# Folding the token transform of the Fourier branch by symmetry

## The chip, the cores and the metric

The kernel runs as one program on 1 core of one Trainium2 chip. Times are device microseconds (us) of one execution, lower is better. TensorE (PE) does the matrix products, VectorE (DVE), ScalarE (ACT) and GpSimd (POOL) the element-wise work, and SyncE (SP) issues the large loads. The engines meet only through semaphores.

## The reference, cut to what matters

The program is one layer of a diffusion trunk over 512 latent tokens of width 1024 (plus 256 context tokens), all in float32. A normalised, modulated input is projected into four branches: global attention, a Fourier branch, windowed attention and a gated recurrence. Each branch result is multiplied by its own matrix, weighted by a gate, and summed; then come an output projection, and a mixture of 16 experts with 2 experts per token. The change touches only the Fourier branch:

```
def fourier_mix(u):                       # u: (1, 512 tokens, 256 features)
    b_, l_, _ = u.shape
    g = u.astype(jnp.float32).reshape(b_, l_, F_GROUPS, F_GROUP_W)     # 4 groups of 64 features
    y = jnp.real(jnp.fft.fft2(g, axes=(1, 3), norm='ortho'))           # tokens and features
    return y.reshape(b_, l_, -1).astype(u.dtype)
...
y_f = fourier_mix(fu)                     # fu: 256 of the columns of h @ w_in
```

The real part of this two-dimensional transform is a sum of two products: for each group the features are multiplied by a 64 x 64 table of cosines and by one of minus sines, and the two results are then multiplied along the tokens by a 512 x 512 table of cosines and one of sines and added.

## The kernel before, in words

Each engine runs a list written out by hand. On TensorE the order is: transposes of the input, first modulation products, the input projection (30 groups of tokens or features by 512 columns, `proj`), the gated recurrence between them, then 32 gate steps. A gate step (`gate`, or `gate_rows` for a part of it) computes one 128-feature block of one branch: eight products of 128x128 by 128x512 for the gate itself, two more for the branch's projection. ScalarE takes the tanh of the gate (`tanh`, L1099), VectorE multiplies it with the branch's projection (`gated`, L1422). Steps 0 to 7 belong to the recurrence's branch, 8 to 15 to the Fourier branch, then come the two attention branches. Steps 0 to 3 run ahead of the Fourier transform, 4 to 6 behind it. Then TensorE transposes queries and keys (`turn`, L463) and goes on to 16 attention units, with the remaining gate steps spread through them, then to the output projection, the router, and 16 experts.

The Fourier transform lies between gate steps 3 and 4, and has two stages on TensorE (all its products are recorded at the helper's line L460):

- First stage, over features: for each of 4 tiles of 128 tokens, the transposed features `fuT` (2 blocks of 128 features by 512 tokens, which stand in `yT[:, 1]`) are the stationary operand, and 256 columns of the constant table `tab` the moving one: 8 products of 256 columns. The result goes to two PSUM banks by turns, and ScalarE copies it (L1010, `copy`) to `gcs`, 4 copies of 128x512.
- Second stage, over tokens: for each of 2 feature blocks, 4 token tiles times 2 tables (cosine, sine) accumulate in one bank: 16 products of 512 columns. The moving operand is `dftL`, the two 512 x 512 tables, 2 MB, which SP loads (L400) as soon as the recurrence is done (`yG_ready`), ahead of the weights of gate steps 4 to 7. ScalarE copies each bank to `yT[:, 1]`.

VectorE's list over the same stretch is a loop of 7 rounds: in rounds 0 to 5 it normalises queries and keys of one token tile (squares, a sum, a root that GpSimd computes at L1694, two multiplications; L1432 to L1436), and in each round it then does `gated(t)`. GpSimd rotates the normalised rows of tiles 0 to 3 (L1715 to L1720) between these roots. TensorE's transposes of queries and keys wait for all of that (`rope_done`, `qk_norm`) and for `yF_ready`. SP's next loads behind `dftL` are the weights of gate steps 4 to 7 and 8 to 11.

What touches the order: a matmul of float32 leaves two records in the trace, a transpose leaves one. Buffers in the arena are reused by hand; `dftL` and `gcs` stand where the recurrence had its scratch rows.

Of the kernel before, what the change touches and what calls it, by code (L numbers as in the profile page):

```python
# [12 lines left out]
ALU = mybir.AluOpType  # L13
# [4 lines left out]
P = 128  # L18
D = 1024
KD = D // P  # L20
SEQ, CTX = 512, 256
XT, CT = SEQ // P, CTX // P
# [20 lines left out]
DFT = LOW + 16  # L43
# [55 lines left out]
def build(nc, A, out):  # L99
    ctx = ExitStack()  # L100
    with ctx:
# [3 lines left out]
        def sem(name):  # L105
            return ctx.enter_context(nc.semaphore(name))


        tab = sb("tab", [P, TABW])
# [27 lines left out]
        def region(at, *shape):  # L137
            n = int(np.prod(shape))
            v = arena[:, at:at + n]
            if len(shape) == 1:  # L140
                return v
            names = "abcd"[:len(shape)]
            return v.rearrange(f"p ({' '.join(names)}) -> p {' '.join(names)}", **dict(zip(names, shape)))

        SLOT = (KD + 2) * CW
        R_RING, R_HT, R_HC, R1 = 0, 15360, 19456, 21504
# [5 lines left out]
        yT = region(R_YT, NB, 2, SEQ)  # L152
        fuT = yT[:, 1]
# [32 lines left out]
        Pr = region(R1, 2, 768)  # L186
        PT = region(R1 + 1536, 2, 768)

        dftL = region(R1, 2, XT, SEQ)
        gcs = region(R1 + 4096, XT, 512)  # L190

        merged = region(R_G + 6656, KD, SEQ)
        th = region(R_HC, 2, SEQ)
# [29 lines left out]
        ps = ctx.enter_context(nc.psum_tensor("ps", [P, 8, 512], F32))  # L223
# [15 lines left out]
        dft_in, wb_in, xr_in, out_done = sem("dft_in"), sem("wb_in"), sem("xr_in"), sem("out_done")  # L239
# [5 lines left out]
        pj_mm, pj_done, qk_zero = sem("pj_mm"), sem("pj_done"), sem("qk_zero")  # L245
# [2 lines left out]
        qkinT_done, qinT_ready, kinT_ready, hgrn1_done = sem("qkinT_done"), sem("qinT_ready"), sem("kinT_ready"), sem("hgrn1_done")  # L248
        kv_done, state_step = sem("kv_done"), sem("state_step")
        att_done, attm_ready, o_done, o_read, yG_ready = sem("att_done"), sem("attm_ready"), sem("o_done"), sem("o_read"), sem("yG_ready")  # L250
        fgc_done, gcs_ready, yF_done, yF_ready = sem("fgc_done"), sem("gcs_ready"), sem("yF_done"), sem("yF_ready")
        qk_norm, rope_done = sem("qk_norm"), sem("rope_done")
        qkT_mm, qkT_ready = sem("qkT_mm"), sem("qkT_ready")
        sc_done, neg_ready, p_ready, ps_ready, pt_mm, pt_act, pt_dve, pv_done, y_copied = (
# [81 lines left out]
        def _(sp):  # L336
# [60 lines left out]
            for n in range(5, second_gate):  # L397
                load(n)
            sp.wait_ge(yG_ready, XT)
            sp.dma_start(dftL, A["dft_long"].rearrange("c (s p) t -> p c s t", p=P)).then_inc(dft_in, 16)  # L400
            load(second_gate)
            load(second_gate + 1)
            load(second_gate + 2)
# [54 lines left out]
        def _(pe):  # L458
            def mm(o, l, r, start, stop):
                return nc.tensor.matmul(o, l, r, start=start, stop=stop, skip_group_check=True)  # L460
# [259 lines left out]
            for g in range(1, 4):  # L720
                gate(g)

            for t in range(XT):
                if t >= 2:
                    pe.wait_ge(gcs_ready, t - 1)
                for ft in range(2):
                    last = mm(ps[:, 2 + 2 * (t % 2), ft * 256:(ft + 1) * 256], fuT[:, ft, t * P:(t + 1) * P],
                              tab[:, DFT:DFT + 256], True, True)
                last.then_inc(fgc_done, 1)
            pe.wait_ge(gcs_ready, XT)  # L730
            pe.wait_ge(dft_in, 16)
            for ft in range(2):
                for s in range(XT):
                    for c in range(2):
                        last = mm(ps[:, 2 + 2 * ft, :], gcs[:, s, ft * 256 + c * P:ft * 256 + (c + 1) * P],
                                  dftL[:, c, s, :], s == 0 and c == 0, s == XT - 1 and c == 1)
                last.then_inc(yF_done, 1)
            for g in range(4, 7):
                gate(g)
# [217 lines left out]
        def _(act):  # L957
# [51 lines left out]
            def copy(o, i):  # L1009
                return A_(o, i, ACT.Copy)  # L1010
# [91 lines left out]
                take_y(j, 2 + 2 * j)  # L1102
            for g in range(4):
                tanh(g)
            for t in range(XT):
                act.wait_ge(fgc_done, t + 1)
                copy(gcs[:, t, :], ps[:, 2 + 2 * (t % 2), :]).then_inc(gcs_ready, 1)
            for ft in range(2):
                act.wait_ge(yF_done, ft + 1)
                copy(yT[:, 1, ft, :], ps[:, 2 + 2 * ft, :]).then_inc(yF_ready, 1)  # L1110
            for g in range(4, 7):
                tanh(g)

# [1 line left out]
            for j in range(7):  # L1115
                act.wait_ge(qkT_mm, j + 1)
                B = ps[:, 2 + j % 2, :]
                if j < 4:
                    last = copy(qT[:, j, :], B)
# [93 lines left out]
        def _(dve):  # L1213
# [203 lines left out]
            def gated(g):  # L1417
                b, half, j, n = gates[g]
                dve.wait_ge(th_ready, g + 1)
                if g >= 10:  # L1420
                    dve.wait_ge(merged_add, g - 9)
                V.scalar_tensor_tensor(merged[:, half * 4 + j, :] if g < 8 else gtmp[:, g % 2, :], th[:, g % 2, :], 1.0,  # L1422
                                       ps[:, gate_bank(g)[0] + 1, :], ALU.add, ALU.mult).then_inc(gm_ready, 1)


            dve.wait_ge(yG_ready, XT)
            for t in range(7):
                if t < NT:
                    dve.wait_ge(pj_done, min(27 + t, len(groups)))
                    X = qk[:, t]  # L1430
                    sq = nsq.rearrange("p (h e) -> p h e", e=HD)
                    link(V.tensor_tensor(sq, X, X, ALU.mult))  # L1432
                    link(V.tensor_reduce(stat[:, 40:52], sq, AX.X, ALU.add))
                    rsqrt(stat[:, 40:52], stat[:, 40:52], 1.0 / HD)
                    link(V.tensor_tensor(X, X, stat[:, 40:52].unsqueeze(2).broadcast_to([P, 12, HD]), ALU.mult))
                    V.tensor_tensor(X, X, gain12[:, :, :], ALU.mult).then_inc(qk_norm, 1)  # L1436
                gated(t)


            def pt_copy(u):  # L1440
# [390 lines left out]
```

## Time and profile before

| what | value |
|---|---|
| median of 3 runs | 935.75 us (933.47 to 936.21) |
| profiled execution, its own time | 938.09 us |
| its span, first to last instruction | 936.1 us |
| mean granted TensorE clock | 0.971 |
| TensorE busy (matmul) | 874.8 us, 93% of the span |
| VectorE / ScalarE / GpSimd busy | 382.1 / 198.7 / 123.4 us |
| read from and written to memory | 128.36 and 12.58 MB |

The profiled execution takes 1.99 us more than its span and lies 2.34 us above the median. Engines overlap, so the busy times don't add up to the span. The whole program ran once for this profile; the rows further down have their starts in us from the start of the span.

### The profile page before, as it was taken

How to read it: one execution, taken by the hardware profiler on the slowest of the kernel's cores; microseconds unless marked ns; L12 is line 12 of the kernel's file. 1: busy time of each engine (PE TensorE's matmuls, PEld its weight loads, DVE VectorE, ACT ScalarE, POOL GpSimd, SP SyncE). 2: the span in 40 equal slices, each digit the busy share in tenths (PEclk: the TensorE clock that was granted, in tenths of full speed). 3: DMA queues.
4: the chain of work that ended last, by engine and by line, in shares of the span. 5: the costliest groups of instructions: out<-in, count | busy, mean ns of one | idle time of the engine just before them, and what ended most of it. 6: DMA issues, size and time to landing. Idle time of an engine off the chain costs nothing. (4 is left out here: it accounts for less than half of the span.)

```text
span 936.1 us, 9796 instructions
## 1 busy us (share of the span) xinstructions
PE 874.8 (93%) x3811; PEld 463.3 (49%) x3811; DVE 382.1 (41%) x795; ACT 198.7 (21%) x436; POOL 123.4 (13%) x109
## 2 busy tenths in 40 slices
PE   4999999999999999999999999999993899999992
PEld 3445475655844445555555554444453444444441
DVE  3239355552445224566576751101336322222221
ACT  3221366100011022223233320010120222111110
POOL 1000000000158200101111011110001022222211
PEclk9899999999999999999999999999995899999997
DMA  8852020300073025252442536204142489999952
GB/s 319 316 191 90 0 90 1 114 1 1 19 296 113 0 90 158 90 164 85 141 144 83 172 132 228 90 0 157 68 142 105 154 261 302 300 285 291 319 138 40
DMA packets 79727, 133.21 MB, mean 142 GB/s; under 512 B 7280, under 2 KB 40256, under 8 KB 79680
## 3 DMA queue, kind: packets, MB, share of 16 engines
q1 hardware_dynamic: 75072, 124.18, 39.0%
q0 software_dynamic: 4608, 8.40, 3.9%
q8 instruction: 30, 0.49, 0.2%
q14 instruction: 17, 0.14, 0.1%
HBM read 128.36 MB, written 12.58 MB: 151 GB/s over the span
## 5 line engine op out<-in xcount | busy, mean ns | idle before, releaser
L460 PE MATMUL ps<-arena 128*128 128x512 f32 (+8 forms) x2974 | 778.2, 451 | 17.2 <-DVE arena L1561 5.7
L460 PEld LDWEIGHTS ps<-arena 128*128 128x128 f32 (+6 forms) x2974 | 362.7, 167 | 383.4 <-issue 361.3
L1010 ACT ACTIVATE arena<-ps 128x128 f32<-128x128 f32 (+2 forms) x133 | 56.0, 445 | 188.9 <-PE ps L460 141.8
L463 PE MATMUL ps<-tab,arena 128*128 128x128 f32 x476 | 68.0, 287 | 13.5 <-DVE arena L1252 5.4
L463 PEld LDWEIGHTS ps<-tab,arena 128*128 128x128 f32 x476 | 58.6, 150 | 41.8 <-issue 34.0
L1422 DVE SCALAR_TENSOR_TENSOR arena<-arena,ps 128x512 f32<-128x512 f32 x32 | 22.0, 687 | 129.4 <-ACT arena L1099 129.2
L1729 POOL TENSOR_TENSOR arena<-arena 128x512 f32<-128x512 f32 x24 | 30.4, 1267 | 279.8 <-DVE arena L1422 279.8
L1694 POOL TENSOR_TENSOR stat<-stat,mhalf 128x1 f32<-128x1 f32 (+2 forms) x20 | 23.2, 1160 | 327.7 <-DVE stat L1227 327.5
L1099 ACT ACTIVATE arena<-ps 128x512 f32<-128x512 f32 x32 | 19.1, 597 | 198.7 <-PE ps L460 198.7
L1652 DVE TENSOR_TENSOR arena<-arena,ps 128x256 f32<-128x256 f32 x16 | 6.7, 421 | 105.9 <-ACT arena L1199 105.9
L1390 DVE SCALAR_TENSOR_TENSOR arena<-arena,cond 128x512 f32<-128x512 f32 x56 | 42.6, 761 | 2.3 <-PE ps L463 0.6
L1466 DVE TENSOR_REDUCE stat<-ps 128x1 f32<-128x768 f32 (+2 forms) x32 | 27.4, 855 | 24.8 <-PE ps L460 24.3
L1757 POOL DMA_INDIRECT out<-arena,tok_of x16 | 25.3, 1582 | 81.8 <-DVE arena L1647 76.0
L1647 DVE SCALAR_TENSOR_TENSOR arena<-ps,gate_of,arena 128x1024 f32<-128x1024 f32 x16 | 20.5, 1284 | 34.7 <-PE ps L460 34.7
L1303 DVE RECIPROCAL arena<-arena 128x256 f32<-128x256 f32 (+1 forms) x14 | 34.1, 2438 | 0.5
L1147 ACT ACTIVATE arena<-ps,stat 128x768 f32<-128x768 f32 (+2 forms) x32 | 25.9, 811 | 30.0 <-DVE stat L1471 29.5
L1748 POOL DMA_INDIRECT arena<-xd,tok_of x16 | 16.8, 1050 | 104.7 <-issue 88.7
L1193 ACT ACTIVATE arena<-ps,modc,A 128x128 f32<-128x128 f32 x64 | 24.1, 456 | 27.2 <-PE ps L463 27.2
L1199 ACT ACTIVATE arena<-ps 128x256 f32<-128x256 f32 x16 | 6.1, 384 | 110.4 <-PE ps L460 110.4
L1368 DVE SCALAR_TENSOR_TENSOR arena<-arena,edec,ps 128x64 f32<-128x64 f32 x92 | 18.2, 274 | 18.0 <-PE ps L460 18.0
L460 PEld LDWEIGHTS ps<-tab,arena 128*128 128x128 f32 x160 | 21.2, 191 | 7.6 <-issue 6.7
L1636 DVE TENSOR_SCALAR arena<-ps,A,modc 128x128 f32<-128x128 f32 x64 | 21.9, 403 | 4.0 <-PE ps L463 3.5
(144 smaller groups left out, 378.4 us busy)
## 6 DMA issues: line engine op xcount, KB each, us to landing
arena<-in_moe_w SPq DMA_DIRECT2D x32, 1024.0 KB, 10.1
arena<-in_w_in SPq DMA_DIRECT2D x12, 2048.0 KB, 8.8
arena<-in_mod_w SPq DMA_DIRECT2D x16, 1024.0 KB, 5.2
arena<-in_moe_w SPq DMA_DIRECT2D x32, 512.0 KB, 10.1
arena<-in_mod_w SPq DMA_DIRECT2D x4, 2048.0 KB, 16.5
arena<-in_w_out SPq DMA_DIRECT2D x2, 2048.0 KB, 8.0
arena<-in_x SPq DMA_DIRECT2D x4, 512.0 KB, 5.2
arena<-in_w_in SPq DMA_DIRECT2D x2, 1024.0 KB, 18.4
```

The lines of the kernel that those rows point to most:

```text
L460: return nc.tensor.matmul(o, l, r, start=start, stop=stop, skip_group_check=True)
L463: return nc.tensor.transpose(o, i, ident[0:n, 0:n])
L1010: return A_(o, i, ACT.Copy)
L1147: A_(Pr[:, a, 0:w], S[:, lo:lo + w], ACT.Exp, bias=stat[:, b3:b3 + 1], scale=SCALE, accum_out=stat[:, b3 + 1:b3 + 2]).then_inc(p_ready, 1)
L1193: last = A_(hgT[:, k, :], ps[:, 0, k * P:(k + 1) * P], ACT.Identity, bias=modc[:, 3 * KD + k, 0:1], scale=A2[:, k:k + 1])
L1303: link(V.reciprocal(e, e))
L1390: last = V.scalar_tensor_tensor(acc, modw[:, k, :], cond[:, k, 0:1], acc, ALU.mult, ALU.add)
L1422: V.scalar_tensor_tensor(merged[:, half * 4 + j, :] if g < 8 else gtmp[:, g % 2, :], th[:, g % 2, :], 1.0, ps[:, gate_bank(g)[0] + 1, :], ...
L1466: link(V.tensor_reduce(stat[:, b3:b3 + 1], S[:, lo:lo + w], AX.X, ALU.max))
L1694: G.tensor_tensor(o, o, mhalf[:, 0:o.shape[1]], ALU.pow).then_inc(root_done, 1)
L1729: G.tensor_tensor(merged[:, ft, :], merged[:, ft, :], gtmp[:, g % 2, :], ALU.add).then_inc(merged_add, 1)
L1757: G.indirect_dma_start(out[0], bass.IndirectOffsetOnAxis(ap=tok_of[:, e:e + 1], axis=0), ys[:, e % 2], None, bounds_check=SEQ - 1, oob_is_ ...
```

## The change

By symmetry of the cosine and the sine about token 256, tokens s and 512 - s are combined before the transform: their sum goes with the cosines, their difference with the sines. And output tokens t and 512 - t need the same two half results, once added, once subtracted. So the tables shrink from 512 x 512 to 256 x 257, and token 256 is carried separately with a table of one row. In the changed kernel:

- SP loads two tables of 256 x 257 and one row of 257, in three DMAs.
- VectorE makes `fold` before its loop (6 instructions), and behind `gated(3)` makes the 512 output tokens from the half results (`unfold`, 4 instructions).
- TensorE's first stage has 8 products of 128 columns and 2 with a single stationary column (token 256); the second has 8 products of 257 columns over 128 rows and 2 of 257 columns over a single row.
- ScalarE copies 3 results of the first stage and 2 even halves of the second (257 columns) instead of 4 and 2 of 512 columns.

```
-        dftL = region(R1, 2, XT, SEQ)
-        gcs = region(R1 + 4096, XT, 512)
+        HALF = SEQ // 2
+        dftL = region(R1, 2, 2, HALF + 1)
+        dftM = region(R1 + 1280, HALF + 1)
+        eL = region(R1 + 1600, 2, HALF + 1)
+        gcM = region(R1 + 3584, 2, P)
+        gcs = region(R1 + 4096, 2, 512)
+        fold = region(R1 + 5120, 2, 2, HALF)
...
             sp.wait_ge(yG_ready, XT)
-            sp.dma_start(dftL, A["dft_long"].rearrange("c (s p) t -> p c s t", p=P)).then_inc(dft_in, 16)
+            for c in range(2):
+                sp.dma_start(dftL[:, c], A["dft_long"][c, 0:HALF, 0:HALF + 1].rearrange("(s p) t -> p s t", p=P)).then_inc(dft_in, 16)
+            sp.dma_start(dftM[0:1, :], A["dft_long"][0, HALF:HALF + 1, 0:HALF + 1]).then_inc(dft_in, 16)
...
-            for t in range(XT):
-                if t >= 2:
-                    pe.wait_ge(gcs_ready, t - 1)
+            pe.wait_ge(fold_ready, 1)
+            for s in range(2):
                 for ft in range(2):
-                    last = mm(ps[:, 2 + 2 * (t % 2), ft * 256:(ft + 1) * 256], fuT[:, ft, t * P:(t + 1) * P],
-                              tab[:, DFT:DFT + 256], True, True)
+                    for c in range(2):
+                        last = mm(ps[:, 2 + 2 * s, ft * 256 + c * P:ft * 256 + (c + 1) * P], fold[:, ft, c, s * P:(s + 1) * P],
+                                  tab[:, DFT + c * P:DFT + (c + 1) * P], True, True)
+                if s == 0:
+                    for ft in range(2):
+                        last = mm(ps[0:1, 3, ft * P:(ft + 1) * P], fuT[:, ft, HALF:HALF + 1], tab[:, DFT:DFT + P], True, True)
                 last.then_inc(fgc_done, 1)
-            pe.wait_ge(gcs_ready, XT)
-            pe.wait_ge(dft_in, 16)
+            pe.wait_ge(gcs_ready, 2)
+            pe.wait_ge(dft_in, 48)
             for ft in range(2):
-                for s in range(XT):
-                    for c in range(2):
-                        last = mm(ps[:, 2 + 2 * ft, :], gcs[:, s, ft * 256 + c * P:ft * 256 + (c + 1) * P],
-                                  dftL[:, c, s, :], s == 0 and c == 0, s == XT - 1 and c == 1)
+                for s in range(2):
+                    mm(ps[:, 2 + 2 * ft, 0:HALF + 1], gcs[:, s, ft * 256:ft * 256 + P], dftL[:, 0, s, :], s == 0, False)
+                mm(ps[:, 2 + 2 * ft, 0:HALF + 1], gcM[0:1, ft, :], dftM[0:1, :], False, True)
+                for s in range(2):
+                    last = mm(ps[:, 3 + 2 * ft, 0:HALF + 1], gcs[:, s, ft * 256 + P:(ft + 1) * 256], dftL[:, 1, s, :], s == 0, s == 1)
                 last.then_inc(yF_done, 1)
...
-            for t in range(XT):
-                act.wait_ge(fgc_done, t + 1)
-                copy(gcs[:, t, :], ps[:, 2 + 2 * (t % 2), :]).then_inc(gcs_ready, 1)
+            for s in range(2):
+                act.wait_ge(fgc_done, s + 1)
+                if s == 0:
+                    copy(gcM[0:1].rearrange("p a n -> p (a n)"), ps[0:1, 3, 0:2 * P])
+                copy(gcs[:, s, :], ps[:, 2 + 2 * s, :]).then_inc(gcs_ready, 1)
             for ft in range(2):
                 act.wait_ge(yF_done, ft + 1)
-                copy(yT[:, 1, ft, :], ps[:, 2 + 2 * ft, :]).then_inc(yF_ready, 1)
+                copy(eL[:, ft, :], ps[:, 2 + 2 * ft, 0:HALF + 1]).then_inc(eL_ready, 1)
...
             dve.wait_ge(yG_ready, XT)
+            dve.wait_ge(pj_done, 26)
+            for ft in range(2):
+                front, back = fuT[:, ft, 1:HALF], fuT[:, ft, SEQ - 1:HALF:-1]
+                V.tensor_copy(fold[:, ft, :, 0:1], fuT[:, ft:ft + 1, 0:1].broadcast_to([P, 2, 1]))
+                V.tensor_tensor(fold[:, ft, 0, 1:HALF], front, back, ALU.add)
+                last = V.tensor_tensor(fold[:, ft, 1, 1:HALF], front, back, ALU.subtract)
+            last.then_inc(fold_ready, 1)
+
+            def unfold(ft):
+
+                dve.wait_ge(eL_ready, ft + 1)
+                odd = ps[:, 3 + 2 * ft, :]
+                V.tensor_tensor(yT[:, 1, ft, 0:HALF + 1], eL[:, ft, :], odd[:, 0:HALF + 1], ALU.add)
+                V.tensor_tensor(yT[:, 1, ft, SEQ - 1:HALF:-1], eL[:, ft, 1:HALF], odd[:, 1:HALF], ALU.subtract).then_inc(yF_ready, 1)
...
                 gated(t)
+                if t == 3:
+                    for ft in range(2):
+                        unfold(ft)
```

## Rows read from the trace of the kernel before

**Rows 1.** Page: busy time, then the granted clock in 40 slices.
```profile
PE 874.8 (93%) x3811; PEld 463.3 (49%) x3811; DVE 382.1 (41%) x795; ACT 198.7 (21%) x436; POOL 123.4 (13%) x109
...
PEclk9899999999999999999999999999995899999997
```

**Rows 2.** Timeline of TensorE, transform and what follows: start, us, what, idle before.
```profile
294.33 3.78 PE L460 MATMUL ps<-tab,arena 128*128 128x256 f32 x16
298.80 39.75 PE L460 MATMUL ps<-arena 128*128 128x512 f32 x92 [0.69 <-ACT arena L1010]
338.39 1.04 PE L463 MATMUL ps<-tab,arena 128*128 128x128 f32 x8
```

**Rows 3.** Timeline of ScalarE, transform's copies and the tanh around them.
```profile
294.22 0.60 ACT L1099 ACTIVATE arena<-ps 128x512 f32<-128x512 f32 x1 [7.99 <-PE ps L460]
...
298.15 0.60 ACT L1010 ACTIVATE arena<-ps 128x512 f32<-128x512 f32 x1 [0.27 <-PE ps L460]
305.97 0.60 ACT L1010 ACTIVATE arena<-ps 128x512 f32<-128x512 f32 x1 [7.22 <-PE ps L460]
312.84 0.60 ACT L1010 ACTIVATE arena<-ps 128x512 f32<-128x512 f32 x1 [6.27 <-PE ps L460]
```

**Rows 4.** Timeline of TensorE, short products elsewhere in the program.
```profile
127.24 1.89 PE L460 MATMUL ps<-arena,tab 128*128 128x256 f32 x8
128.97 0.95 PE L460 MATMUL ps<-tab,arena 128*128 128x4 f32 x8
...
579.08 1.95 PE L460 MATMUL ps<-tab,arena 128*128 128x128 f32 x16
580.87 17.33 PE L460 MATMUL ps<-arena 128*128 128x512 f32 x40
```

**Rows 5.** Timeline of ScalarE, two copies of 256 columns in a row.
```profile
95.41 0.38 ACT L1010 ACTIVATE arena<-ps 128x256 f32<-128x256 f32 x1 [6.42 <-PE ps L460]
95.69 0.38 ACT L1029 ACTIVATE arena<-ps 128x256 f32<-128x256 f32 x1
```

**Rows 6.** Timeline of TensorE over one attention unit.
```profile
367.32 1.47 PE L463 MATMUL ps<-tab,arena 128*128 128x128 f32 x12
...
380.36 1.47 PE L463 MATMUL ps<-tab,arena 128*128 128x128 f32 x12
```

**Rows 7.** Timeline of VectorE, before and during its loop.
```profile
253.77 0.42 DVE L1414 TENSOR_TENSOR arena<-arena 128x256 f32<-128x256 f32 x1
...
269.10 0.69 DVE L1422 SCALAR_TENSOR_TENSOR arena<-arena,ps 128x512 f32<-128x512 f32 x1 [8.31 <-ACT arena L1099]
...
296.32 0.96 DVE L1435 TENSOR_TENSOR arena<-arena,stat 128x768 f32<-128x768 f32 x1 [5.33 <-POOL stat L1694]
...
322.05 0.69 DVE L1422 SCALAR_TENSOR_TENSOR arena<-arena,ps 128x512 f32<-128x512 f32 x1 [12.77 <-ACT arena L1099]
...
328.17 0.96 DVE L1436 TENSOR_TENSOR arena<-arena,gain 128x768 f32<-128x768 f32 x1
```

**Rows 8.** Timeline of GpSimd, the root behind the last rotation.
```profile
305.02 2.27 POOL L1694 TENSOR_TENSOR stat<-stat,mhalf 128x12 f32<-128x12 f32 x1
```

**Rows 9.** SP's timeline, then DMA queues and issues (count, KB, us to landing).
```profile
254.22 0.37 SPq L400 DMA_DIRECT2D arena<-in_dft_long  x1
...
q1 hardware_dynamic: 75072, 124.18, 39.0%
...
arena<-in_dft_long SPq DMA_DIRECT2D x1, 2048.0 KB, 8.7
```

**Rows 10.** Windows around the router: busy us per engine, granted clock, DMA share.
```profile
698.00:702.00 4.00, 4.00 (x20) 4.00 (x20) 2.82 (x10) 2.02 (x6) 0.06 (x1) 0.50 1.10 359
...
732.00:736.00 4.00, 4.00 (x10) 1.71 (x9) 0.00 (x0) 0.00 (x0) 0.00 (x0) 0.99 1.07 373
```

**Rows 11.** TensorE's timeline beside that stretch.
```profile
699.73 6.85 PE L460 MATMUL ps<-rw,arena 128*128 128x16 f32 x32
...
727.80 9.23 PE L460 MATMUL ps<-arena 128*128 128x512 f32 x16 [1.24 <-ACT arena L1193]
```

More of the change, by code:

```diff
@@ L250, in build @@
         att_done, attm_ready, o_done, o_read, yG_ready = sem("att_done"), sem("attm_ready"), sem("o_done"), sem("o_read"), sem("yG_ready")
-        fgc_done, gcs_ready, yF_done, yF_ready = sem("fgc_done"), sem("gcs_ready"), sem("yF_done"), sem("yF_ready")
+        fold_ready, fgc_done, gcs_ready = sem("fold_ready"), sem("fgc_done"), sem("gcs_ready")
+        yF_done, eL_ready, yF_ready = sem("yF_done"), sem("eL_ready"), sem("yF_ready")
         qk_norm, rope_done = sem("qk_norm"), sem("rope_done")
```

## The prediction, made before the changed kernel ran

> **What bounds the kernel now.** I read the page's busy times first: TensorE is busy 874.8 of 936.1 us, VectorE 382.1, and the granted clock is near full in all slices but one, around 700 to 725 us [rows 1]. So the time is TensorE's list, and what matters is how long TensorE spends in the transform and whether anything makes it wait there. TensorE's timeline answers the first: the first stage starts at 294.33, the second at 298.80 after an idle 0.69 us that ScalarE's last copy ended [rows 2, 3]. The second has 16 products of 512 columns. The distance of its two copies gives the price: 312.84 - 305.97 = 6.87 us for 8, 0.858 us each [rows 3]; a gate step, 10 of them, is 8.58. So gate step 4 starts at 298.80 + 16 x 0.858 = 312.53, and the transform takes 18.20 us. From there to 338.39 TensorE does nothing but gate steps [rows 2]: 312.53 + 3 x 8.58 = 338.27 confirms the price. What is saved before 312.53 is saved on the path, if nobody is late.
>
> **TensorE, first stage.** The 256-column product costs (128.97 - 127.24) / 4 = 0.4325 us (8 records, two to a product) [rows 4]. The 128-column product costs (580.87 - 579.08) / 8 = 0.224 us, and its last result comes 0.16 us after the next one starts (1.95 - 1.79) [rows 4]. The new stage has 10 of these. The last of the six of its first half is issued by 294.33 + 6 x 0.224 = 295.67, the stage by 296.57.
>
> **The products with one column or one row** have no row of their own. Their columns are priced as any other (0.224 and 0.4325). What is open is the change between a whole array and a part of it. An attention unit holds three such changes (whole array, 64 rows for the scores, 64 columns for the values, whole again). It lasts 380.36 - 367.32 = 13.04 us [rows 6]. Its parts: 12 transposes 1.31 (1.47 less 0.16 of tail), 10 gate products of 512 columns 8.58, scores 0.858 + 0.4325 (the two heads side by side), values 6 x 0.224 = 1.34: together 12.52. The rest, 0.52 us, over three changes is 0.17 us each. The new stages have two changes around the single column and four around the single rows. Low end: 0, if they are hidden. High end: 0.5 each, the 0.31 us that a 512-column product's result came behind its last issue (305.97 - 298.80 - 8 x 0.858) [rows 2, 3] plus the 0.17. I take 0.17, the only row that holds such a change: 0.35 us in the first stage, 0.69 in the second.
> The Trainium skill, "TensorEngine Tiling (Array Packing)", section Key Properties, says that changing the tiling mode drains TensorE. It gives no time; this trace's 0.17 us agrees with it in kind. Without that rule the sum would be 1.0 us better.
>
> **ScalarE between the stages.** The six products end at 295.67 + 0.35 + 0.16 = 296.18. The tanh of step 3 is over at 294.82 [rows 3], so ScalarE is free. A copy of 256 columns holds the next one off by 0.28 us (95.69 - 95.41) [rows 5]; gcM at 296.18, the first gcs at 296.46, over before the second half's results arrive at 296.57 + 0.35 + 0.16 = 297.08. The second gcs copy takes 0.60, and TensorE goes on 0.05 behind it, as before (298.15 + 0.60 = 298.75, then 298.80) [rows 2, 3]. The second stage starts at 297.73 instead of 298.80: 1.07 us.
>
> **TensorE, second stage.** 10 products of 257 columns, 0.434 each with one column more (0.4325 x 257/256): 4.34, plus 0.69 for the changes: 5.03. It ends at 302.76 instead of 312.53.
>
> **Sum: 312.53 - 302.76 = 9.8 us** on the path (10.8 with changes of the array free, 7.8 with 0.5 each).
>
> **What is added beside the path, and who could be late:**
> - *fold on VectorE.* Four operations of 255 elements at 0.42 [rows 7] and two of one element, which I bound by 0 and 0.42: 1.7 to 2.5 us, and some 0.3 between them. It can start at 254.2, as its input is ScalarE's copy of groups 24 and 25, long behind. It ends by 257.1, TensorE asks for it at 294.3: 37 us of cover. Even if reading backwards made it ten times dearer it would end by 282. It delays the norm of tile 0, behind which VectorE idled 8.31 us until 269.10 [rows 7], so it ends there.
> - *unfold on VectorE.* It stands behind gated(3), which was late, 298.2 to 298.9 (296.32 plus two of 0.96, then 0.69), as the norm ahead of it waited 5.33 us for GpSimd's root, and the tanh was over at 294.82 [rows 3, 7]. Half result 0 leaves TensorE at 297.73 + 2.17 + 0.35 + about 0.2 = 300.4, ScalarE's copy ends at 300.8, the two VectorE operations at about 301.8; half result 1 leaves at 303.0 and is unfolded by 304.3. The norm of tile 4, which began at 298.8, so begins 5.5 us later. But its root at GpSimd ran only from 305.02, behind the last rotation, [rows 8], and is now asked for at 304.3 + 2.1 = 306.4: root over at 308.7, norm over at 310.8. gated(4) can't start before the tanh of step 4, 302.76 + 8.58 + 0.3 + 0.6 = 312.2. Tile 5's norm ended 328.17 + 0.96 - 322.05 = 7.1 us after gated(4) started [rows 7], so at about 319.3. TensorE asks for it at 302.76 + 3 x 8.58 = 328.5. Cover left: 9 us; without it each us would be lost at the transposes. The rotation of tile 3 ends before 305.02, as it did [rows 8].
> - *SP.* Three issues instead of one, 0.37 us each plus gap [rows 9]: the next weights go out 0.8 us later, but 1.5 MB less stand ahead of them. Gate step 4 needs them at 302.8, 47 us after their issue; the old table's load landed in 8.7 us.
> - ScalarE: two 512-column copies less, smaller ones; never last except as above. Gate steps 5 and 6 need gated(3) and gated(4), at 298.9 and 312.9, against TensorE's 318.2 and 326.8 (behind the eight gate products): covered.
>
> **Time.** 938.09 - 9.8 = 928.3 us for an execution like the profiled one. It lay 2.34 us above the median, so against the median: 935.75 - 9.8 = 926.0 us, if everything behind 312.5 moves forward as a block.
>
> **Rivals.**
> 1. *The clock's phases move.* The granted clock was 0.50 at 698 to 702 and 0.99 again from 732, by the page's slices low in between [rows 1, 10]. TensorE was busy at the low level (1.2 GHz) over the router's products up to 706.58, and again from 724, with 16 records in 9.23 us [rows 11] where 8 products at full level would take 6.87. When the clock falls and rises need not move with the program. If it fell only behind the router, up to 8.6 / 2 = 4.3 us would be gained; if it rose before 727.80, 2.4; if it rose only behind those 16 records, 13.73 - 9.23 = 4.5 would be lost. Likely sizes are half of that: 923.6 to 928.5, extremes 922 to 930.5. For: the clock fell in the midst of busy time. Against: VectorE and the DMAs set most of that stretch.
> The Trainium skill's "TensorE: Matmul & The Clock Gate", part 1, says that the gate doesn't reset with the kernel; this would make the time wander by run, the three runs shown spread over 2.7 us.
> 2. *VectorE becomes last at the transposes.* If unfold and the norms behind it took 9 us more than worked out, the gain would be given back at 328.5, and the time be 935.75. For: VectorE's list was already behind at gated(3). Against: four operations at 0.42.
> 3. *Slower: the tables arrive late.* Rows of 257 elements are an odd length. If each element were moved singly, 2 x 256 x 257 = 131,584 packets would go out. The profile's packets took 0.390 x 16 x 936.1 / 75072 = 0.078 us of an engine each [rows 9], so 640 us over 16 engines, and the time would be over 1500. Small packets may be far cheaper; the change turns slower than before where the table lands after 297.7 + 9.8 = 307.5, that is from 53 x 16 / 131,584 = 6.5 ns a packet. At 8 ns it would land at 320 and the time be 948. Against: the rows are contiguous on both sides, like those of the old table, which landed 2 MB in 8.7 us [rows 9]; as whole rows, 512 packets at 0.078 / 16 take 2.5 us.
> The Trainium skill's "DMA: Bandwidth & Descriptors" has a rule that a non-contiguous last dimension costs a descriptor per element, and one that a transfer's engines follow from its slowest dimension: neither would slow the two large tables here (128 partitions, contiguous rows), and the one-row table is a single short row.
>
> **Chances.** Forecast with its own bounds (7.8 to 10.8 off, 925.0 to 928.0) 0.71; rival 1 beyond these bounds 0.21, still faster; rival 2 0.04; rival 3 0.04. A measurement of this kernel tells about 0.3% (2.8 us) from no change; both first cases are beyond it. So faster 0.92, same 0.04, slower 0.04. Range: 922.3 to 929.8, the bounds of the changes of the array with rival 1's likely sizes and the spread of the runs.
>
> **What would show it.** On TensorE: 16 records of 257 columns over 128 rows and 4 over one row; gate step 4 starting near 302.8 and the transposes near 328.6, with no idle time ended by VectorE or a DMA. On ScalarE, the second gcs copy ending near 297.7. On VectorE, fold over by 257 and the last norm by 320. The router's clock row, moved by 10 us, shows rival 1. I am wrong if TensorE waits for `fold`, `yF_ready` or `qk_norm`, or if the products with a single row cost much over 0.6 us.

## The result, and the profile after

| | median | runs | ratio to before, 95% interval |
|---|---|---|---|
| before, measured beside it | 935.98 us | 4 (933.47 to 936.83) | |
| changed kernel | 927.08 us | 4 (924.14 to 928.33) | 0.9904 [0.9884, 0.9925] |
| the same again (e8) | 928.63 us | 5 | 0.9917 [0.9901, 0.9933] |
| the same again (e9) | 927.86 us | 6 | 0.9923 [0.9897, 0.9949] |

The change makes the kernel faster by 8.9 us, about 1% (926.0 us was forecast, 922.3 to 929.8). In two later series of runs, each with the kernel before measured beside it, it was 7.3 us (before: 935.90) and 7.1 us (before: 934.92). The profiled execution took 927.07 us with a span of 925.2.

The timeline of TensorE after, the rows that answer to [rows 2] (start, us, what, idle before):

```profile
294.58 2.75 PE L468 MATMUL ps<-tab,arena 128*128 128x128 f32 x20
298.01 31.14 PE L468 MATMUL ps<-arena 128*128 128x257 f32 x80 [0.69 <-ACT arena L1022]
328.99 1.04 PE L471 MATMUL ps<-tab,arena 128*128 128x128 f32 x8
```

From the transform's first product to the transposes of queries and keys it is 34.41 us, where it was 338.39 - 294.33 = 44.06. That is 9.65 us less. The idle 0.69 us in the middle is still there and still ends with ScalarE. ScalarE's timeline, the answer to [rows 3]:

```profile
294.47 0.60 ACT L1111 ACTIVATE arena<-ps 128x512 f32<-128x512 f32 x1 [7.99 <-PE ps L468]
296.27 0.85 ACT L1022 ACTIVATE arena<-ps 1x256 f32<-1x256 f32 x2 [1.21 <-PE ps L468]
297.36 0.60 ACT L1022 ACTIVATE arena<-ps 128x512 f32<-128x512 f32 x1 [0.24 <-PE ps L468]
300.88 0.39 ACT L1022 ACTIVATE arena<-ps 128x257 f32<-128x257 f32 x1 [2.92 <-PE ps L468]
303.44 0.39 ACT L1022 ACTIVATE arena<-ps 128x257 f32<-128x257 f32 x1 [2.17 <-PE ps L468]
312.02 0.60 ACT L1111 ACTIVATE arena<-ps 128x512 f32<-128x512 f32 x1 [8.20 <-PE ps L468]
```

The first row is the tanh of gate step 3, the last that of step 4. Step 4's ten products take 8.58 us, and their last result comes 0.31 us later, so they start at 312.02 - 8.89 = 303.13, and the second stage took 5.12 us. VectorE, the answer to [rows 7], at the end of `fold`, at the two halves of `unfold`, and at the last multiplication of the last norm:

```profile
255.63 0.42 DVE L1446 TENSOR_TENSOR arena<-arena 128x255 f32<-128x255 f32 x1
...
301.30 0.42 DVE L1453 TENSOR_TENSOR arena<-arena,ps 128x257 f32<-128x257 f32 x1 [2.18 <-ACT arena L1022]
...
304.20 0.41 DVE L1454 TENSOR_TENSOR arena<-arena,ps 128x255 f32<-128x255 f32 x1
...
318.78 0.96 DVE L1465 TENSOR_TENSOR arena<-arena,gain 128x768 f32<-128x768 f32 x1
```

`fold` is over at 256.1, 38 us ahead of its use. The last norm is over at 319.7, 9.2 us ahead of the transposes.

Each trace can be cut at five rows of TensorE: the transform's first product, the first transpose of queries and keys, the router's second group of 16 records, the experts' first product, the end of the span. The differences of these starts, in us:

| kernel | to the transform | transform to transposes | to the router | router to experts | to the end | span |
|---|---|---|---|---|---|---|
| before | 294.33 | 44.06 | 355.73 | 33.68 | 208.30 | 936.1 |
| changed | 294.58 | 34.41 | 355.72 | 33.31 | 207.18 | 925.2 |
| changed (e8) | 297.83 | 34.40 | 355.74 | 33.51 | 207.72 | 929.2 |
| changed (e9) | 294.87 | 34.40 | 355.75 | 33.52 | 207.46 | 926.0 |

Only the second column is the change's. The stretch from the transposes to the router repeats to 0.03 us. What wanders is the start (3.3 us between executions of one and the same program) and the experts.

### The profile page after: what moved, and what is told of

It reads as the page before. It is cut to its first block and busy times, and to the rows that moved or that the text cites. A ratio compares the mean times of both kernels' runs of the same rounds, so it can differ in the third digit from the quotient of the medians.

```text
span 925.2 us, 9791 instructions
## 1 busy us (share of the span) xinstructions
PE 865.7 (94%) x3803; PEld 459.7 (50%) x3803; DVE 383.7 (41%) x805; ACT 197.6 (21%) x435; POOL 122.8 (13%) x109
## 5 line engine op out<-in xcount | busy, mean ns | idle before, releaser
L468 PE MATMUL ps<-arena 128*128 128x512 f32 (+9 forms) x2962 | 770.6, 451 | 15.1 <-DVE arena L1593 5.7
L468 PEld LDWEIGHTS ps<-arena 128*128 128x128 f32 (+5 forms) x2962 | 360.3, 167 | 375.9 <-issue 355.2
L1022 ACT ACTIVATE arena<-ps 128x512 f32<-128x512 f32 (+5 forms) x132 | 54.7, 439 | 180.3 <-PE ps L468 133.3
L471 PEld LDWEIGHTS ps<-tab,arena 128*128 128x128 f32 x476 | 58.0, 148 | 42.7 <-issue 34.3
L468 PEld LDWEIGHTS ps<-tab,arena 128*128 128x128 f32 (+1 forms) x164 | 20.6, 189 | 7.4 <-issue 6.9
## 6 DMA issues: line engine op xcount, KB each, us to landing
arena<-in_moe_w SPq DMA_DIRECT2D x32, 512.0 KB, 10.7
```

The source lines that it names most:

```text
L471: return nc.tensor.transpose(o, i, ident[0:n, 0:n])
```

## The experiments

**e1, half of the fold: input tokens folded, output tokens not.**

```
-dftL = region(R1, 2, 2, HALF + 1); dftM = region(R1 + 1280, HALF + 1)
+dftL = region(R1, 2, 2, SEQ);      dftM = region(R1 + 2048, SEQ)
 ...
-mm(ps[:, 2 + 2 * ft, 0:HALF + 1], ...)   # even; odd in bank 3 + 2 * ft; unfold on VectorE
+mm(ps[:, 2 + 2 * ft, :], ...)            # all five accumulate in one bank, 512 columns
-copy(eL[:, ft, :], ps[:, 2 + 2 * ft, 0:HALF + 1]).then_inc(eL_ready, 1)
+copy(yT[:, 1, ft, :], ps[:, 2 + 2 * ft, :]).then_inc(yF_ready, 1)
```

> Input tokens folded as in the changed kernel, output tokens not: tables of 256 x 512, 10 products of 512 columns in the second stage, no unfold on VectorE. Theory (the gain is columns streamed by TensorE, all of it passed on to the end): the second stage costs 10 x 0.858 + 4 changes of the array at 0.17 to 0.19 = 9.3 us instead of 5.1, so gate step 4 starts 4.2 us later than in the changed kernel; time 927.1 + 4.2 = 931.3, between before and after. Rival (the gain comes from the lighter load or the clock's phases, not from columns): about 927. Rival (unfold on VectorE costs on the path): below 927 + 4.2 by the unfold's 1.7 us or more.

Measured: 930.58 us (931.3 expected), ratio 0.9936 [0.9914, 0.9957], beside 936.38 for before. The timeline of TensorE:

```profile
294.31 2.75 PE L468 MATMUL ps<-tab,arena 128*128 128x128 f32 x20
297.74 35.38 PE L468 MATMUL ps<-arena 128*128 128x512 f32 x80 [0.69 <-ACT arena L1022]
332.96 1.04 PE L471 MATMUL ps<-tab,arena 128*128 128x128 f32 x8
```

From the first product to the transposes it is 38.65 us, 4.24 more than the changed kernel's. The theory had 4.2. So of the 9.65 us, 5.4 come from folding the input tokens and 4.25 from folding the output tokens, both as columns streamed.

**e2, 1.5 MB of unused loads put back.**

```
+for a in range(3):
+    if a:
+        sp.wait_ge(dft_in, 48 + 16 * a)
+    sp.dma_start(spare, A["dft_long"][:, 0:P, :].rearrange("c p t -> p c t")).then_inc(dft_in, 16)
...
-pe.wait_ge(dft_in, 48)
+pe.wait_ge(dft_in, 96)
```

> The changed kernel, which also loads 1.5 MB it doesn't use (three loads of 512 KB into a spare place, one after the other, ahead of the gate weights, and TensorE waits for them at the second stage). Theory (the lighter load brought nothing): SP is held back by some 5 to 10 us at 255 to 270, TensorE's rows at the transform stay as they are, time 927 within the spread. Rival (part of the 8.9 us gained is the load's): later by up to the 1.1 us that the transform's own rows don't explain, or a new idle row of TensorE ended by a DMA.

Measured: 926.41 us, ratio 0.991 [0.988, 0.9941]; the changed kernel had 0.9904. SP issued the next weights at 263.35 instead of 255.77. The transform took 34.40 us, and no wait of TensorE there ends with a DMA. No gain of the lighter load is seen, in the rows or in the time.

**e3, the products with one column or one row made with the whole array.** The part of token 256 is not computed, so only the transform's rows are read, not the time.

```
-last = mm(ps[0:1, 3, ft * P:(ft + 1) * P], fuT[:, ft, HALF:HALF + 1], tab[:, DFT:DFT + P], True, True)
+last = mm(ps[:, 3, ft * P:(ft + 1) * P], fuT[:, ft, HALF:HALF + P], tab[:, DFT:DFT + P], True, True)
...
-mm(ps[:, 2 + 2 * ft, 0:HALF + 1], gcM[0:1, ft, :], dftM[0:1, :], False, True)
+mm(ps[:, 2 + 2 * ft, 0:HALF + 1], gcs[:, 0, ft * 256:ft * 256 + P], dftL[:, 0, 0, :], False, True)
```

> The products with one column or one row are replaced by products of the same columns over the whole array on other data (the middle token's part is not computed). Theory (a change between whole and partial array costs 0.17 us, six of them on the path): the first stage's 20 records take 2.40 instead of 2.75 us, the second stage 4.34 instead of 5.12, so gate step 4 starts 1.1 us earlier. Rival (the extra time is that of the single-row products themselves, or a cost of 257 as an odd length, whatever the array): the stages stay at 2.75 and 5.1 us.

```profile
292.14 2.47 PE L468 MATMUL ps<-tab,arena 128*128 128x128 f32 x20
295.29 30.36 PE L468 MATMUL ps<-arena 128*128 128x257 f32 x80 [0.69 <-ACT arena L1022]
325.49 1.04 PE L471 MATMUL ps<-tab,arena 128*128 128x128 f32 x8
```

The same number of products and columns take 33.35 us, 1.06 less; six changes less, so 0.18 us a change (0.28 of it in the first stage, 0.78 in the second). So the length of 257 costs nothing of its own. Whether the 1.06 us belong to the changes between whole and partial array or to the four partial products themselves, e3 can't say, as it takes out both; e7 below parts them.

**e4, token 256 left out.** Neither its products nor the copy of gcM are there, nor its part of the result.

```
-if s == 0:
-    for ft in range(2):
-        last = mm(ps[0:1, 3, ...], fuT[:, ft, HALF:HALF + 1], ...)
-mm(ps[:, 2 + 2 * ft, 0:HALF + 1], gcM[0:1, ft, :], dftM[0:1, :], False, True)
-if s == 0:
-    copy(gcM[0:1].rearrange("p a n -> p (a n)"), ps[0:1, 3, 0:2 * P])
```

> The middle token is left out: no product with one column or one row, no copy of gcM. Theory: first stage 8 x 0.224 + 0.16 = 1.95 us (from 2.75), second 8 x 0.434 = 3.47 (from 5.12); ScalarE's last copy starts 0.8 us earlier, so gate step 4 is 2.45 us earlier than in the changed kernel. Rival (ScalarE's copy ahead of the first gcs copy sets the second stage's start): the second stage starts more than 0.8 us earlier.

Transform to transposes: 324.18 - 292.14 = 32.04 us, 2.37 less than the changed kernel's, with 2.45 expected. The second stage starts 2.71 us after the first here and 3.43 in the changed kernel: 0.72, so the copy of gcM held nothing up. The single token 256 costs 2.4 us of TensorE, nearly half of it the 1.06 us of e3.

**e5 and e6, how much cover VectorE has.** 6 and 16 unused operations behind `unfold`:

```
+for _ in range(6):        # e6: 16
+    link(V.tensor_tensor(nsq, nsq, nsq, ALU.min))
```

> The changed kernel with 6 idle operations of 768 elements (0.98 us each, 5.9 us) on VectorE behind unfold. Theory (VectorE's last norm ends at 319.7, TensorE asks at 329.0, 9.2 us of cover): the norm of tile 4 and gated(4) come later, the last norm ends near 324, TensorE's transposes still start near 329.0 with no idle row ahead of them. Rival (what VectorE does behind the transform is already on the path): transposes later by up to 5.9 us.

> The same with 16 such operations, 15.7 us. Theory: unfold ends 304.6, tile 4's norm starts at 320.3 and takes 6.3 with the root, gated(4) 0.7, tile 5's norm 6.3: last norm ends at 333.5 to 333.8, TensorE's transposes start 4.5 to 5 us later than 329.0, behind an idle row of that length ended by VectorE (L1465 or its line here). So the cover runs out at 9 to 10 us. Rival (the transposes wait for GpSimd's rotation or unfold instead): no such row.

With 6, the last norm ends at 324.56 + 0.96 = 325.5, still 5.0 us ahead of TensorE's transposes, and these start 34.41 us after the transform's first product, as without. With 16, VectorE's row of the last multiplication, and TensorE's of the transposes:

```profile
332.79 0.96 DVE L1465 TENSOR_TENSOR arena<-arena,gain 128x768 f32<-128x768 f32 x1
```

```profile
327.41 1.98 PE L468 MATMUL ps<-arena 128*128 128x512 f32 x4 [0.18 <-DVE arena L1436]
333.85 6.13 PE L471 MATMUL ps<-tab,arena 128*128 128x128 f32 x28 [4.46 <-issue]
```

The transform to transposes takes 39.47 us, 5.06 more. The idle row is there, 4.46 us, but it is put down to "issue" and not to VectorE as I had written; that it ends just behind VectorE's row (333.75) shows who is late. Another 0.18 us goes at gate step 6, which waits for gated(4). 15.9 us of work cost 5.1, so 10.8 us were covered: 9.2 ahead of the transposes, and most of the rest in the 1.58 us for which VectorE otherwise idles ahead of gated(4), until the tanh of step 4 is done.

The late transposes cost more than their 5.06 us. From them to the router this trace takes 691.08 - 333.85 = 357.23 us, 1.5 more than in every other trace (355.72 to 355.77), because the granted clock fell to 0.50 (the lower of its two levels, 1.2 GHz) during the idle 4.46 us and stayed there over the transposes. A window just behind the idle time (busy us by engine, then granted clock and DMA share):

```profile
334.00:336.00 2.00, 2.00 (x10) 1.77 (x11) 0.94 (x2) 0.77 (x2) 0.00 (x0) 0.50 0.00 0
```

**e7, a reordered version.** The products of token 256 with one column first, those with one row right behind the first stage:

```
+for ft in range(2):
+    last = mm(ps[0:1, 3, ft * P:(ft + 1) * P], fuT[:, ft, HALF:HALF + 1], tab[:, DFT:DFT + P], True, True)
+last.then_inc(fgc_done, 1)
 pe.wait_ge(fold_ready, 1)
 ...                                                  # first stage, as before, without token 256
+even, odd = (5, 2), (3, 4)
+for ft in range(2):
+    pe.wait_ge(gcs_ready, 1 + ft)
+    mm(ps[:, even[ft], 0:HALF + 1], gcM[0:1, ft, :], dftM[0:1, :], True, False)
+pe.wait_ge(gcs_ready, 3)
 ...                                                  # the other 8 products
```

> The products with one column go first (they need no fold), those with one row stand directly behind the first stage, in a bank that is free, so that they run while ScalarE copies gcs; even halves in banks 5 and 2, odd ones in 3 and 4. Theory: four changes of the array instead of six, and the idle 0.69 us (0.85 with the tail) is filled: 10 x 0.224 + 10 x 0.434 + 4 x 0.18 = 7.3 us from the first product to gate step 4, instead of 8.55; time 1.2 us less than the changed kernel. Rival (ScalarE is last anyway): the four-row products' time is saved but the wait for gcs moves behind them, gain 0.3 to 0.9.

> The changed kernel again beside the kernel before and the last experiment: theory 9.0 to 10.0 us below before (9.65 us by TensorE's rows at the transform, give or take what the router's and experts' stretch adds from run to run). Rival (the profile's 10.9 us of span is the true gain): 10.5 or more.

```profile
296.13 2.58 PE L468 MATMUL ps<-tab,arena 128*1 128x128 f32 x20 [0.15 <-PE ps L468]
298.64 30.55 PE L468 MATMUL ps<-arena 1*128 1x257 f32 x80
329.03 1.04 PE L471 MATMUL ps<-tab,arena 128*128 128x128 f32 x8
```

There is no idle row left between the stages; the transform to transposes takes 32.90 us, 1.5 less than the changed kernel's, where 1.2 were expected.

This also settles what e3 left open. From the transform's first product to gate step 4 it takes 32.90 - 25.86 = 7.04 us (25.86 is the changed kernel's 328.99 - 303.13 behind that point), and the columns alone take 10 x 0.224 + 10 x 0.434 = 6.58. So 0.46 us are left for the same four partial products, where e3 had found 1.06: the price is that of the changes of the array, now four, and not of the products. The single records say the same. The four of the two single-row products start at 298.64, 298.96, 299.17 and 299.39, the next, of the whole array, at 299.70 and 300.02: 0.22 apart where nothing changes, as whole-array records of 257 columns are, and 0.31 and 0.32 at a change.

But the medians of e7 and e8 were 924.55 and 928.63, 4.1 us apart, more than the transform has to give, and the changed kernel itself was only 7.3 us below before, less than its rows and less than the 9 to 10 that e8 had been expected to show. So both were run again.

> The changed kernel a third time, to part what it gains from what wanders. Its transform took 34.4 us in both traces (44.06 before), the rest of the program between 890.8 and 894.8. Theory (the rest wanders by chance): transform to transposes again 34.4 us, the first product anywhere from 292 to 298 us; time 7 to 11 us below before. Rival (the changed kernel's start is later by itself): first product at 294.6 or later again, and time only 7 to 8 us below.

> The reordered version a second time: its transform to transposes took 32.90 us, 1.5 us less than the changed kernel's 34.40. Theory (the 4.1 us between the two medians hold 2.6 us of chance): again 32.9 us there, and a median 1 to 2.5 us below the changed kernel's of this call. Rival (the new order gives 4 us): 4 us below again, with a row elsewhere that shows the other 2.6 in both traces.

927.86 and 924.18 us: 3.7 us apart again, and 34.40 and 32.90 us at the transform again. The expectation of 1 to 2.5 us was wrong. The changed kernel's first product came at 294.87, and it was 7.1 us below before, which e9's rival also allows (294.6 or later, 7 to 8 us). But e1 to e6, whose lists on TensorE are the changed kernel's up to there, reached it after 292.14 to 296.07 us, with before's 294.33 in the middle, so the traces don't speak for a start that is late by itself. The missing 2.8 us stand at the router, in both traces of the reordered version. The router's last 32 records in the changed kernel, in e9 and in e10:

```profile
690.04 6.86 PE L468 MATMUL ps<-rw,arena 128*128 128x16 f32 x32
```

```profile
690.62 6.85 PE L468 MATMUL ps<-rw,arena 128*128 128x16 f32 x32
```

```profile
687.88 3.90 PE L468 MATMUL ps<-rw,arena 128*128 128x16 f32 x32
```

Windows of e10 over this stretch (busy us by engine, then granted clock and DMA share) say why:

```profile
684.00:688.00 4.00, 3.54 (x20) 3.14 (x21) 2.19 (x6) 1.98 (x6) 1.49 (x3) 0.57 1.04 347
688.00:692.00 4.00, 3.78 (x33) 3.67 (x31) 1.63 (x6) 1.69 (x5) 0.00 (x0) 0.91 1.07 376
692.00:696.00 4.00, 0.00 (x0) 0.00 (x0) 3.62 (x12) 0.04 (x1) 0.00 (x0) 0.50 0.74 301
```

The clock was at 1.2 GHz for most of 684 to 688, over the transposes, came back for the router's products, and fell again just before the last of them ended (0.91 over 688 to 692). In before it fell once and stayed low over all of them [rows 10, 11]. The change of state is the same in kind, but it lies elsewhere against the work.

**e11 and e12, more work ahead of it.** Was it the new order, or only how much work lies ahead of the router? Two unused products of 512 columns ahead of the transform, in the reordered version (e11) and in the changed kernel (e12):

```
+for _ in range(2):
+    mm(ps[:, 2, :], tab[:, DFT:DFT + P], hT[:, 0, :], True, True)
```

> The reordered version with 2 unused products of 512 columns ahead of the transform (1.7 us), so that from its start to the transposes it takes 34.6 us, as long as the changed kernel (34.4). In both traces of the reordered version the router's last 32 records took 3.9 to 4.0 us, mostly at the full clock, and 30.6 us passed from the router's first row before them to the experts; in three traces of the changed kernel and in that of before they took 6.85 us, at half, and 33.3 to 33.7. Theory A (where the clock falls at the router hangs on how much work lies ahead of it): the records take 6.85 again, the stretch 33.3 or more, median 924.2 + 1.7 + 2.8 = 928.7. Theory B (it is the new order itself, or chance): 3.9 again, 925.9.

> The changed kernel with the same 2 unused products: 36.1 us from the transform's first product of the padding to the transposes. If the router's stretch stays long (6.85 us for its last 32 records), the median is 928.0 + 1.7 = 929.7. If the length of the work ahead decides (theory A), it may turn short here, and the median be 928.0 + 1.7 - 2.8 = 926.9: more work, less time. Theory B gives 929.7 in any case.

Measured: e11 929.26 us (928.54 to 929.90), ratio 0.9937 [0.9921, 0.9952]; e12 926.07 us (923.27 to 927.81), ratio 0.99 [0.9881, 0.9919]. With 1.9 and 1.7 us more work, e11 lost 4.7 to 5.1 us against the medians of e7 and e10 (the intervals are apart), and e12 came out 1.0 to 2.6 below the three medians of the changed kernel (the intervals overlap; by the two stretches in the traces it gains 2.8 - 1.7 = 1.1). The router's last 32 records, in e11 and in e12:

```profile
690.60 6.85 PE L468 MATMUL ps<-rw,arena 128*128 128x16 f32 x32
```

```profile
690.58 4.30 PE L468 MATMUL ps<-rw,arena 128*128 128x16 f32 x32 [0.28 <-DVE arena L1551]
```

And the clock in one window of each:

```profile
688.00:692.00 4.00, 3.17 (x16) 3.17 (x16) 3.19 (x9) 2.54 (x8) 0.93 (x2) 0.50 1.09 361
```

```profile
688.00:692.00 4.00, 2.73 (x23) 2.31 (x22) 3.57 (x11) 3.01 (x8) 1.30 (x3) 1.00 1.08 363
```

Theory A had forecast 928.7 and 926.9 us, and longer records in the one, shorter ones in the other; both medians came within 0.8 us of it and the records as it said. Theory B had 925.9 and 929.7, and both lie outside the measured runs. So it is the length ahead and not the new order by itself. In e12 the clock stayed full until some 1.4 us before the end of the router's products (0.69 in the window 692 to 696), and didn't fall twice as in the reordered version. The five stretches, cut as above:

| kernel | to the transform | transform to transposes | to the router | router to experts | to the end | span |
|---|---|---|---|---|---|---|
| e7, reordered | 296.13 | 32.90 | 355.74 | 30.59 | 208.44 | 923.8 |
| e10, reordered | 293.65 | 32.90 | 355.74 | 30.76 | 207.55 | 920.6 |
| e11, reordered + 2 | 294.48 | 34.78 | 355.73 | 33.63 | 208.58 | 927.2 |
| e12, changed + 2 | 293.51 | 36.12 | 355.73 | 30.69 | 205.55 | 921.6 |

In all fourteen traces the router's stretch is either 30.6 to 30.8 or 33.3 to 33.8 us, and in all of them the length ahead says which: short at 32.0 us of transform (e4, 30.67), 32.9, 32.9 and 33.35 (e3, 30.82), long at five times 34.4 (e2 33.69, e5 33.79) and at 34.8, short at 36.1, long again at 38.65 (e1, 33.53), 39.5 (e6, 33.75) and 44.06. Each run has one trace; in its other executions the router wasn't seen.

The Trainium skill, "TensorE: Matmul & The Clock Gate", part 1, says that the gate's observation doesn't restart with the kernel and so its moments vary from run to run. At the start of the program this case agrees (292.14 to 297.83 us to the transform in fourteen traces). At the router it shows little: by the granted clock of 688 to 692 us (0.61 in the changed kernel's first trace, 0.52 in e9's) the fall came some 4.2 and 3.1 us behind the router's row at 684.71 and 685.02, and all five traces with 34.4 us of transform had the long stretch.

The reordered version beats the kernel before: 924.55 and 924.18 us, ratios 0.987 [0.9848, 0.9892] and 0.9883 [0.9859, 0.9908]. Against the changed kernel the intervals are apart in e7 and e8 and overlap a little in e9 and e10. By the traces it gains 11.2 us at the transform and 2.9 to 3.1 at the router against the one trace of before, 14.1 to 14.3 in all; the medians gained 11.4 and 10.7. That gap of some 3 us is taken up below.

## Why the prediction was right, point by point

- *TensorE's list bounds the kernel, and what the transform saves goes through to the end.* Right up to the router: 34.40 us in all three traces of the changed kernel, and what lies behind unchanged to 0.03 us. e1 and e4 moved it by what their columns cost. Of the 9.65 us, 0.7 to 2.6 are missing in the medians; see what stays open.
- *First stage.* 294.58 to 298.01 is 3.43 us; the sum had 3.40 (294.33 to 297.73). The second gcs copy started at 297.36; shifted by the later start (0.25), the sum had 297.33.
- *Changes of the array.* 0.17 us worked out from one attention unit; e3 measured 0.18 over six, e7 0.12 over its four. Without this term the forecast would have been 10.8 and off by 1.2 on the path. The Trainium skill's rule ("TensorEngine Tiling (Array Packing)", Key Properties) that a change of the tiling mode drains the engine agrees in kind: the records of e7 stand 0.09 to 0.11 us further apart at the changes.
- *Second stage.* 5.12 us, 5.03 in the sum: 0.19 a change rather than 0.17.
- *Sum on the path.* 9.65 measured, 9.8 forecast.
- *fold and unfold are covered.* Right. Reading and writing backwards cost nothing: 0.42 us for 255 elements as for 256 [rows 7]. The two single-element copies of `fold` took 0.17 and 0.16. `unfold` ended at 304.6, 304.3 in the sum; the cover was 9.2 us, 9 in the sum, and e5 and e6 put its end between 5.9 and 15.9 us of added work, by e6's sum at 10.8.
- *Rival 3, tables late.* Didn't occur: TensorE's only wait at the second stage ended with ScalarE, as before.
- *Rival 1, the clock.* Between before and after it hardly mattered at the router, 33.68 and 33.31 us. But its mechanism was there, and I had it half wrong: at the router it is not loose from the program. It goes with the length of the work ahead, and is worth 2.8 us. The likely sizes named there, 923.6 and 928.5, are also a little off: halves of 4.3 and 4.5 give 923.9 and 928.3.
- *The time.* 926.0 forecast, 927.08 measured. With its own bounds (925.0 to 928.0) the sum covers this and e9's 927.86 but not e8's 928.63; that one is inside the range only because the clock had been given room. That the first series lay 1.1 us from the forecast, where the later ones lay 2.6 and 1.9, is in part luck.

**What stays open.** The rows give 9.65 us, the three series gave 8.9, 7.3 and 7.1. The three intervals share 0.9901 to 0.9925, a gain of 7.0 to 9.3 us; 9.65 us is 0.9897, which is in the first, at the edge of the third and outside the second. The reordered version shows a gap of the same sign, 3 us. The span and the mean granted clock of nearly every execution are known, and an estimate from them says that the gap is the clock's. It counts all time at the lower level as if TensorE had been busy in it. Span times clock, what the span would be at the full clock throughout, is on average 908.4 us over 46 executions of before, 898.5 over 15 of the changed kernel and 897.5 over 12 of the reordered version: 9.8 and 10.9 us less, against 9.65 and 11.2 by the rows (the averages are good to some 0.5 us). The time at the lower level, 2 x (1 - clock) x span, is 50.8, 55.1 and 49.7 us. So the changed kernel ran 4.2 us longer at half clock than before did and lost about half of that, 2.1 us, again: 9.8 - 2.1 = 7.7 us, the difference of the average spans. The one trace of before, with a mean clock of 0.971 and so 54.3 us at the lower level, was slower by the clock than most, so a total taken against that trace alone comes out too large. Whether before's other executions had more of the full clock at the start, the router or the experts isn't settled.

## What to carry to other kernels

Price a fold or any algebraic saving on TensorE by columns streamed, then add a change between whole and partial array for each odd piece, and put these odd pieces together and into a wait that is there anyway: 1.5 us here for nothing but order, 0.85 of it the wait and the rest the changes. Cut the traces of both kernels at the same rows before reading a total; a total that moves by more than the cut stretch points to the clock elsewhere. And where a clock stretch lies behind the change, a few padded variants tell what the total owes to it: 1.9 us of added work cost the reordered version 5 us, and 1.7 us cost the changed kernel nothing that could be measured. Where the mean clock of each execution is known, compare span times clock as well: one trace of each kernel needn't be typical.

## What the runs showed of the hardware that I had not expected

- The router's last 32 records took the same 6.84 to 6.86 us in all five traces of kernels with 34.4 us of transform, and changed when 1.7 or 1.9 us of work were added 390 us ahead of them, in both directions: 6.85 to 4.30 us and 3.90 to 6.85 us.
- An idle time of 4.46 us on TensorE (e6) was followed by a stretch at 1.2 GHz that cost 1.5 us more.
- TensorE reached the transform after 292.14 to 297.83 us; in the changed kernel alone 294.58 to 297.83. The mean granted clock from 15 us on goes with it. In the changed kernel's first trace (1 - 0.74) x 20 = 5.2 us of full clock are missing, in e8 (1 - 0.61) x 22 = 8.6, 3.4 us more for a start that is 3.25 later:

```profile
15.00:35.00 20.00, 16.03 (x67) 6.89 (x67) 5.99 (x14) 4.69 (x8) 1.35 (x3) 0.74 1.04 389
```

```profile
15.00:37.00 22.00, 17.19 (x69) 8.15 (x68) 6.01 (x15) 4.57 (x8) 1.64 (x3) 0.61 1.04 389
```

- A product with a single row costs its columns in full (records 0.22 us apart in e7, as with 128 rows); only the changes around it come on top. Its records stand as 1*128 in the lines by shape of the changed kernel from 293 to 304 us, where every one of them is beside a change (count, busy us, mean ns of one):

```profile
L468 PE MATMUL ps<-arena 128*128 128x257 f32 x16 | 4.3, 399 | 0.7 <-ACT arena L1022 0.7
...
L468 PE MATMUL ps<-arena 1*128 1x257 f32 x4 | 1.4, 427 | 0.0
```
